# Full-array products in attention, a seven-product down projection, and a split join in a two-layer mixer block

## What is computed

```
p = modulate(rms_norm(x)) @ w_in                 # split into branches A, B, C, D and gates
A: grouped attention, 8 query heads of 64 on 2 key/value heads, rotary positions
B: latent attention, 8 heads, keys and queries of 64 + 32 columns, values of 64
C: a recurrent scan (WKV), forward and backward, computed in chunks of 64 tokens
D: 8 heads of 64, neighbourhood attention with a bias among latents, plus the context
   scores = q @ k^T * scale;  p = softmax(scores);  o = p @ v          # in A, B and D
x = x + gate1 * (sum_i sigmoid(g_i) * (o_i @ w_branch_i)) @ w_out
x = x + gate2 * (relu(modulate(rms_norm(x)) @ w_mlp1) ** 2) @ w_mlp2
```

## Time and profile before

| | us |
|---|---|
| median of 3 runs | 2406.4 (2401.82 to 2408.03) |
| profiled execution | 2408.26 |
| its span, first to last instruction | 2406.5 |
| TensorE busy | 2362.7 |
| VectorE busy | 1075.4 |
| ScalarE busy | 602.9 |
| GpSimd busy | 348.2 |

### The profile page before, as it was taken

The page is one execution under the profiler, slowest core; times in us unless marked ns, Lnnn a source line. Parts: engine busy times, 40 slices in busy tenths (PEclk is TensorE's granted clock), DMA queues, the critical chain, the costliest instruction groups (busy, mean ns, idle before and its releaser), DMA issues.

```text
span 2406.5 us, 48804 instructions
## 1 busy us (share of the span) xinstructions
PE 2362.7 (98%) x21774; PEld 1617.1 (67%) x21774; DVE 1075.4 (45%) x1988; ACT 602.9 (25%) x1248; POOL 348.2 (14%) x249
## 2 busy tenths in 40 slices
PE   8999999999999999999999999999999999999998
PEld 5554564455556554458888887566577767788887
DVE  3452334243555542137876875431546566421101
ACT  3353323132232321011000002441333334211100
POOL 0000000000101100026666671010000011000000
PEclk9999999999999999999999999999999999999999
DMA  8101111213231113232224565112121212245443
GB/s 307 53 18 70 45 61 44 96 63 110 95 107 39 45 46 115 78 123 97 88 88 149 189 243 194 53 71 89 53 89 64 64 61 66 81 149 175 155 152 105
DMA packets 64543, 239.99 MB, mean 100 GB/s; under 512 B 7024, under 2 KB 8064, under 8 KB 63440
## 3 DMA queue, kind: packets, MB, share of 16 engines
q1 hardware_dynamic: 61824, 220.23, 26.6%
q0 software_dynamic: 2512, 16.66, 1.9%
HBM read 235.81 MB, written 1.05 MB: 98 GB/s over the span
## 4 chain that ended last, share of the span: by engine, by line
PE 89%; DVE 5%; DMA 2%; issue 1%; ACT 1%; SPq 0%; DVEq 0%; ACTq 0%
PE psum L430 87%; PE psum L769 2%; DMA normed<-panels 1%; DVE normed L2348 1%; DVE normed L2345 1%; DMA arena<-panels 1%; DVE arena L2329 0%; SPq L2712 0%; ACT arena L811 0%; DVE arena L1492 0%; ACT normed L719 0%; ACT arena L821 0%; DVE arena L1509 0%; DVE arena L1507 0%; DVE arena L1235 0%
## 5 line engine op out<-in xcount | busy, mean ns | idle before, releaser
L430 PE MATMUL psum<-normed,panel_ring 128*128 128x256 f32 (+1 forms) x2880 | 973.5, 484 | 3.0 <-DVE arena L1235 1.1
L430 PEld LDWEIGHTS psum<-normed,panel_ring 128*128 128x128 f32 x2880 | 530.2, 190 | 318.9 <-issue 265.8
L430 PE MATMUL psum<-arena 64*64 64x64 f32 (+6 forms) x14040 | 608.2, 251 | 20.1 <-issue 9.0
L430 PEld LDWEIGHTS psum<-arena 64*64 64x64 f32 (+3 forms) x14040 | 431.6, 139 | 251.6 <-issue 180.9
L430 PE MATMUL psum<-arena,panel_ring 128*128 128x256 f32 (+1 forms) x2048 | 550.4, 422 | 0.0
L430 PEld LDWEIGHTS psum<-arena,panel_ring 128*128 128x128 f32 x2048 | 384.3, 190 | 125.2 <-issue 81.4
L786 DVE TENSOR_REDUCE softmax_stats<-psum 128x1 f32<-128x512 f32 (+1 forms) x144 | 83.7, 599 | 171.6 <-PE psum L430 170.3
L811 ACT ACTIVATE arena<-psum,softmax_stats 128x512 f32<-128x512 f32 (+1 forms) x144 | 87.6, 612 | 211.8 <-PE psum L769 102.5
L1235 DVE SCALAR_TENSOR_TENSOR arena<-arena,psum 128x512 f32<-128x512 f32 (+1 forms) x64 | 35.3, 553 | 152.8 <-PE psum L430 145.3
L1220 ACT ACTIVATE arena<-psum 128x512 f32<-128x512 f32 (+1 forms) x64 | 31.4, 490 | 216.1 <-PE psum L430 216.0
L1728 POOL COPY arena<-arena 128x512 f32<-128x512 f32 x16 | 21.3, 1356 | 440.8 <-PE psum L430 431.1
(11 more groups left out here) (215 smaller groups left out, 1872.5 us busy)
## 6 DMA issues: line engine op xcount, KB each, us to landing
panel_ring<-panels SPq DMA_DIRECT2D x350, 512.0 KB, 3.5
normed<-panels SPq DMA_DIRECT2D x40, 512.0 KB, 3.7
arena<-panels SPq DMA_DIRECT2D x24, 512.0 KB, 12.0
arena<-small_b POOLq DMA_DIRECT2D x2, 2176.0 KB, 8.9
arena<-bias_d POOLq DMA_DIRECT2D x2, 2048.0 KB, 8.9
arena<-x_t SPq DMA_DIRECT2D x2, 1024.0 KB, 7.1
arena<-x_t POOLq DMA_DIRECT2D x1, 2048.0 KB, 10.6
arena<-const_r POOLq DMA_DIRECT2D x2, 800.0 KB, 6.3
```

What stands on the lines that cost most here:

```text
L430: return nc.tensor.matmul(out, lhsT, rhs, start=start, stop=stop, skip_group_check=check)
```

## The change

1. Attention. The keys of A and the queries of D exist twice, once with zeros in the rows of head 1 and once with zeros in those of head 0 (`a_k1`, `d_q1`), and a score product runs over all 128 rows. VectorE makes A's second key in the normalisation stage; ScalarE makes D's two query tiles with a per-partition scale (`head_scale`) that is zero in one half. The two value products of a key tile become one, with both heads' value columns as stationary side and both heads' probabilities as 512 moving columns; of its result each head's own quarter is copied out, by two VectorE copies. B's scores stay as they are.
2. Down projection of layer 1 (`stage_mlp_down7` for `stage_mlp`). The up projection stays. The hidden tiles are laid out as 16 groups of seven parts; 16 units of two panels each have 7 x 4 products of 128 columns. GpSimd makes three weight sums of a unit, VectorE two; a join of four output quarters follows every fourth unit.
3. Branch C. The join has one step more: state products of one kind, a yield, state products of the other kind, `h_full`, and then the products for the outputs. In the plan half of a step's fillers are placed before the neighbouring pair's `close` and `prep` instructions.

```diff
-                        for i in range(2):
-                            p = mm(psum[heads[i], 4 + g % 2, :CTX], v_of(t, i, kt), probT[:, g % 2, i, kt, :], kt == 0, kt == nk // P - 1)
+                        p = mm(psum[:, 4 + g % 2, :], v_of(t, kt), probT[:, g % 2, :, kt, :], kt == 0, kt == nk // P - 1)
...
-                    nc.vector.tensor_copy(out[:, t, half * CTX - col0:(half + 1) * CTX - col0], psum[:, 4 + g % 2, :CTX]).then_inc(out_free.h, 1)
+                    for i in range(2):
+                        p = nc.vector.tensor_copy(out[heads[i], t, half * CTX - col0:(half + 1) * CTX - col0],
+                                                  psum[heads[i], 4 + g % 2, i * CTX:(i + 1) * CTX])
+                    p.then_inc(out_free.h, 1)
...
+                if s == 0:
+                    nc.vector.memset(other[:64, :], 0.0)
...
+                    if j == 1:
+                        nc.vector.tensor_copy(other[64:, :CTX], k[64:, :CTX])
+                        nc.vector.tensor_tensor(t[:64], t[:64], turned[:64], ALU.add)
+                        link(e, nc.vector.tensor_tensor(other[64:, CTX:], t[64:], turned[64:], ALU.add))
+                        nc.vector.memset(k[64:, :], 0.0).then_inc(rotated.h, 1)
...
-                    nc.scalar.activation(q[:, j, :], ps[:, :nq], ACT.Copy, scale=HD ** -0.5).then_inc(b.free.h, 1)
+                    if j == 0:
+                        e.wait_ge(rotated[0].h, rotated[0].at(rotated[1]))
+                        e.wait_ge(up_done[0].h, up_done[0].at(up_done[1]))
+                    nc.scalar.activation(q[:, j, :], ps[:, :nq], ACT.Identity, scale=head_scale[0])
+                    nc.scalar.activation(at["d_q1"][:, j, :], ps[:, :nq], ACT.Identity, scale=head_scale[1]).then_inc(b.free.h, 1)
...
-            e.wait_ge(gq_ready.h, gq_ready.at(1))
-            for c in y_chunks:
-                for d, hd in units:
-                    t = tside(d, hd)
-                    mm(yb[d][half[hd], token(c)], pu[t, d, c, 1, :], m4[t, d, c, :], False, False, check=True)
             for n, (src, right) in enumerate(((kt, vt), (bt, pu[:, :, :, 1, :]))):
+                if n == 0:
+                    e.wait_ge(gq_ready.h, gq_ready.at(1))
...
-            p.then_inc(h_full.h, 1)
-            yield
+                if n == 1:
+                    p.then_inc(h_full.h, 1)
+                    for c in y_chunks:
+                        for d, hd in units:
+                            t = tside(d, hd)
+                            mm(yb[d][half[hd], token(c)], pu[t, d, c, 1, :], m4[t, d, c, :], False, False, check=True)
+                yield
...
+                between = n // 2 if (p and tick < CLOSE) or (p < PAIRS - 1 and tick > RAW + LEVEL_STEPS) else 0
+                fill(others, between)
...
-                fill(others, n)
+                fill(others, n - between)
```

The core of the new down projection, TensorE's part of a unit and the sums that it waits for:

```diff
+                e.wait_ge(weights.h, weights.at(3 * u + 1))
+                product(u, bank(v, 0)[:, 1, :], x2, 0, opens(u))
+                e.wait_ge(shared.h, shared.at(2 * u + 1))
+                product(u, bank(v, 1)[:, 0, :], x5, 3, opens(u))
+                p = product(u, bank(v, 0)[:, 0, :], w1[:, 0:4, :], 1, False, begins=True)
...
+                e.wait_ge(shared.h, shared.at(2 * u + 2))
+                product(u, bank(v, 2)[:, 0, :], w1[:, 4:8, :], 6, opens(u))
+                e.wait_ge(weights.h, weights.at(3 * u + 3))
+                p = product(u, bank(v, 1)[:, 1, :], w2[:, 4:8, :], 2, False, begins=True)
...
+                p = product(u, bank(v, 2)[:, 1, :], w2[:, 0:4, :], 5, False)
...
+                product(u, m1_bank(v), x1, 4, opens(u)).then_inc(m1_done.h, 1)
...
+            if u >= 2:
+                e.wait_ge(m1_done.h, m1_done.at(u - 1))
...
+                nc.gpsimd.tensor_tensor(wx[:, u % 2, 1], w2[:, 0:4, :], w2[:, 4:8, :], ALU.add).then_inc(weights.h, 1)
+                nc.gpsimd.tensor_tensor(w2[:, 0:4, :], w2[:, 0:4, :], w1[:, 0:4, :], ALU.subtract).then_inc(weights.h, 1)
+                nc.gpsimd.tensor_tensor(wx[:, u % 2, 0], w1[:, 0:4, :], w2[:, 4:8, :], ALU.add).then_inc(weights.h, 1)
...
+                nc.vector.tensor_tensor(wx[:, u % 2, 2], w1[:, 0:4, :], w1[:, 4:8, :], ALU.add).then_inc(shared.h, 1)
+                e.wait_ge(shared.h, shared.at(2 * u + 1))
+                nc.vector.tensor_tensor(w1[:, 4:8, :], w1[:, 4:8, :], w2[:, 4:8, :], ALU.subtract).then_inc(shared.h, 1)
```

More of the change, by code:

```diff
@@ L371, in build @@
     eps, gn_eps = gc[:, G_EPS:G_EPS + 1], gc[:, G_EPS + 1:G_EPS + 2]
+    head_scale = [gc[:, G_EPS + 2 + i:G_EPS + 3 + i] for i in range(2)]
     def carve(at, *shape):
@@ L1980, in pe, with product @@
-            sum_up(e)
+            def product(u, out, lhs, part, opening, begins=False):
+                for k in range(4):
+                    p = mm(out, lhs[:, k, :], hid[:, 4 * (u % 4) + k, part, :], opening and k == 0, closes(u) and k == 3, check=True)
+                    if begins and k == 0:
+                        p.then_inc(panels_begun.h, 1)
+                return p
+            for u in range(NU):
+                at_first = P_DOWN + 8 * (u // 4) + u % 4
+                loaded[u] = stream.take(l, at_first), stream.take(l, at_first + 4)
@@ new lines, in pe, with arrived @@
+            e.wait_ge(added.h, added.at(KT - 3))
+            token_sums(6, h[:, 0, tok], n, True)
+            e.wait_ge(squared.h, squared.at(KT - 1))
+            token_sums(6, h[:, KT - 2, tok], n, False)
+            e.wait_ge(squared.h, squared.at(KT))
+            token_sums(6, h[:, KT - 1, tok], n, False).then_inc(sums_full.h, 1)
+            yield
+        def arrived(e, u):
+            for _, slot_in, n_in in loaded[u]:
+                e.wait_ge(slot_in.h, n_in)
+            if u >= 2:
+                e.wait_ge(m1_done.h, m1_done.at(u - 1))
@@ new lines, in pool @@
+        def pool(e):
+            yield from idle(8 * N_UP)
+            for u in range(NU):
+                (w1, _, _), (w2, _, _) = loaded[u]
+                arrived(e, u)
+                nc.gpsimd.tensor_tensor(wx[:, u % 2, 1], w2[:, 0:4, :], w2[:, 4:8, :], ALU.add).then_inc(weights.h, 1)
+                nc.gpsimd.tensor_tensor(w2[:, 0:4, :], w2[:, 0:4, :], w1[:, 0:4, :], ALU.subtract).then_inc(weights.h, 1)
+                nc.gpsimd.tensor_tensor(wx[:, u % 2, 0], w1[:, 0:4, :], w2[:, 4:8, :], ALU.add).then_inc(weights.h, 1)
+                yield
@@ L2003, in dve, with residual_of @@
+                if j in (29, 31):
+                    weight_sums((j - 29) // 2)
                 yield
             e.wait_ge(mod_ready[l].h, mod_ready[l].at(4))
-            for m in range(KT):
-                if m >= 2:
-                    add(e, m - 1)
-                residual(e, outs, m, l, lambda m, s: mod[:, l, 40 + m, s:s + 1], tok, None)
+            def residual_of(m, s, c):
+                return nc.vector.scalar_tensor_tensor(x[:, m, (left, right)[s]], c, mod[:, l, 40 + m, 1:2], x[:, m, (left, right)[s]],
+                                                      ALU.mult, ALU.add)
@@ L2009, in dve @@
+            for u in range(NU):
+                if closes(u) and u == NU - 1:
+                    join(u // 4)
+                if u + 2 < NU:
+                    weight_sums(u + 2)
+                if closes(u) and u < NU - 1:
+                    join(u // 4)
                 yield
             yield
-        return Stage(f"mlp{l}", 8 * N_UP + KT + 1, pe=pe, act=act, dve=dve), sums_full, (outs.full, KT)
+        return Stage(f"mlp{l}", 8 * N_UP + NU + 1, pe=pe, act=act, dve=dve, pool=pool), sums_full, (emptied, ND)
@@ L2021, in stage_mlp7 @@
         inputs, weights, m1_done, hid_ready = (sem("mlp_" + a, t) for a, t in (
[L2022 removed]
+            ("vector_sums", 5), ("weights", 10 * NU), ("m1_done", 2 * NU), ("hidden", NU)))
         m3_full, m4_full, m67_full, m3_copied, m67_copied, emptied = (sem("mlp7_" + a, NU + ND) for a in (
@@ L2640, in layer @@
         else:
-            stage, sums, loadable = stage_mlp(l, tok, at["hid"], at["relu"], ready, at["rstd"])
+            stage, sums, loadable = stage_mlp_down7(l, tok, at, ready)
             place(stage, 12)
```

146 lines of the change are left out of this document (112 added, 34 removed).

## The result

The changed kernel takes 2465.7 us (median of 4 runs, 2461.66 to 2470.15) against 2407.2 for the kernel before (4 runs): +58.5 us, ratio 1.0248, 95% interval 1.0225 to 1.0272. The forecast was 2457 us in a range of 2446 to 2468. The time lies in the range. It is 8.7 us above the forecast, and +58.5 us over the kernel before where the forecast's sum gave +48.8.

A forecast was written before the change was run, and what follows sets the result against it. TensorE's instruction stream was taken as the bound, busy 2362.7 of 2406.5 us. Terms 61.5 + 1 - 3 - 9.95 + 0.7 - 1.5 = +48.8 us on the profiled 2408.3 gave 2457 us, range 2446 to 2468.

The forecast's parts named there:

- attention, from whole cycles: Attention of both layers: full products instead of packed pairs lengthen the cycles of A, B and D, +61.5 us in sum.
- normalisation stage's extra instructions: Normalisation before attention, both layers: work queued behind A's second-key memsets delays TensorE, +1 us (0 to 4).
- waits that the longer stream fills: Attention, above all A: the longer TensorE stream fills idle gaps, 1.7 us in each layer, -3 us (0 to -6).
- down projection with its tail: Layer 1: 896 narrower records instead of 110.55 us give -9.95 us, the longer tail +0.7 us.
- split join, fillers in between: Branch C: both edits remove waits of TensorE at the scan and in the merges, -1.5 us (-5 to +3).
- the tail: After layer 1's down projection: the last join's added additions and residuals delay the last square, +0.7 us (0 to +1.5).
- The rival of binding weight sums: Down projection of layer 1: GpSimd's sums at 2.25 us each set the pace, +10.5 us, 2468 us; chance 0.12.
- nearly as now: Branch C: TensorE's waits at the scan's state update, 3.2 us before, were to stay about the same.
- the likeliest case alone: Whole kernel: the forecast with its own terms' bounds and no rival, 2450 to 2464 us; chance 0.74.

The follow-up runs named there:

- e8: The changed kernel without the split join and without the fillers in between: 2463.9 us, ratio 1.0249 to the kernel before.
- e10: The changed kernel with its split join but with the fillers placed as before: 2457.5 us, ratio 1.0223 to the kernel before.
- e4: The kernel before with the split join and the fillers in between, together and alone: 2409.9 us, ratio 1.0023.
- e2: The kernel before with the zero-padded scores of A and D alone, values still packed pairs: 2424.5 us, ratio 1.0086.
- e5: The kernel before with only the two loops around the packed value products swapped, all of head 0 first: 2424.6 us, ratio 1.0085.
- e1: The kernel before with the value products alone as full products, scores still packed pairs: 2458.3 us, ratio 1.0220.
- e3: The kernel before with the seven-product down projection of layer 1 alone: 2398.1 us, ratio 0.9969.
- e11: The kernel before with the seven-product down projection, all five weight sums of a unit on GpSimd: 2390.4 us in one run.
- e6: The kernel before with the split join and its added step alone, fillers placed as before: 2404.6 us, ratio 1.0001.
- e7: The kernel before with half of a step's fillers placed before the neighbour pair's instructions, join as before: 2414.7 us, ratio 1.0038.

## Why the prediction was right, and where it was off

| step | predicted us | measured us |
|---|---|---|
| attention, from whole cycles | +61.5 | +61.8 (e8, stages +36.0 and +25.8), all three rows together; +60.9 in e10 |
| normalisation stage's extra instructions | +1 | not seen: 52.0 us from the first norm of layer 1 to the first row maximum, before 52.1 |
| waits that the longer stream fills | -3 | -0.3 (waits for the exponentials, 1.2 before, 0.9 after) |
| down projection with its tail | -9.25 | -9.2 (the whole last stage) |
| split join, fillers in between | -1.5 | +3 to +8 (e4) |
| sum | +48.8 | +57.1 (spans), +58.5 (medians) |

**Attention.** The mechanism is shown, not only argued. A pair of products in different halves of the array overlaps in time, and a full product does not make up for it: the cycles of D and B came out at 30.10 and 30.13 us in layer 0, 17.21 and 12.95 in layer 1, against the forecast 30.11, 30.11, 17.21 and 12.93; e2 shows that zeros save nothing, e5 that the gain lies in the order of the stream. Pricing whole cycles instead of single stretches was what made it exact, since the entries and exits of the packed stretches were thus in the sum: ten fillers take 4.39 us before a packed score (e1, 416.37 to 420.76) and 4.29 before a full one (e1, 259.40 to 263.69), and four transposes 0.49 behind a packed stretch and 0.44 behind a full one. The change saved these, and they are small beside what it lost. The Trainium skill's page TensorEngine Tiling (Array Packing), Key Properties, says that a change of tiling mode drains the engine, without a figure. The 0.1 us agree with it in kind; that they are this drain no run here shows.

**The waits that would be filled** were filled by 0.3 us instead of 3, a miss of 2.7 us. One wait of 0.32 us in A of layer 1 is gone (1535.42 before). The cycle of A in layer 0, where TensorE waits for ScalarE's exponentials, still has its two, 0.57 and 0.29 us before, 0.61 and 0.30 after; the first of them before, then both after:

```profile
123.70 3.01 PE L430 MATMUL psum<-arena 64*128 64x512 f32 x20 [0.57 <-ACT arena L811]
```

```profile
125.84 5.42 PE L433 MATMUL psum<-arena 128*128 128x512 f32 x12 [0.61 <-ACT arena L816]
...
147.85 5.42 PE L433 MATMUL psum<-arena 128*128 128x512 f32 x12 [0.30 <-ACT arena L816]
```

The cycle went from 18.37 to 22.01 us, +3.64, even more than the 3.44 of D. A score product waits until the exponentials of the item before it are done. From the start of that item's scores to the end of the first wait it was 4.01 us before (119.69 to 123.70) and 4.23 after (121.61 to 125.84): the chain grew by 0.22 us, and the scores at its head by 0.23 (0.63 to 0.86). A longer product fills a wait only if it does not lie on the chain that is waited for, and here it did. Nor were all of the 1.7 us of gaps that the term was taken from such waits: 0.57 and 0.29 are, another 0.55 in the same 60 us waits for L1050, a square in branch B.

**The down projection** was right in sum: the body gave 0.5 us more than forecast (100.6 forecast, 100.05 measured), and the tail took a little more (+0.7 forecast, +0.9 to the last square, +1.1 to the square root of the final norm). The row of another stage with the same shape, 0.1123 us a record, carried over to 0.6% (0.1117). The rival of binding weight sums fell, in e3 and, in its hard form, in e11.

**The split join and the fillers** is the step that failed in sign: "I take -1.5 us", measured +3 to +8 (e4). The prediction looked at the waits which the edits might remove, and not at the stage whose instructions they move: with the fillers split, half of the cover that stood behind the next pair's preparation went in front of it. e6 has the join at -2 to +2 us, e7 the fillers at +6 to +12, and in e10, which undoes them in the changed kernel, the stretch with attention of layer 1 is 2.9 us shorter. The waits at the scan's state update, forecast "nearly as now", went from 3.2 to 6.1 us in the changed kernel. The prediction's upper bound for this term was +3. That the total still fell into the range owes something to the range's width, 2446 to 2468, which had been opened upwards for the weight sums, a rival that did not come; the likeliest case alone ended at 2464, under the measured 2465.7.

**What stays open:** how much of the fillers' cost is waits at the tanh (3.4 us in e7's span) and how much spells of lower clock in the first pair; what the join itself costs within 2 us; and why e8, without the join, is 6 us slower by the medians than e10 with it, where e6 finds no effect of the join. The intervals of e8 and e10 overlap, and of the 5.4 us between their profiled spans 3.9 lie ahead of the second norm of layer 0, 1.1 in the MLP of layer 0 and 0.5 in layer 1; the first of these stretches varies as much without an edit.

## What to carry to other kernels

Where TensorE is the bound, two products of half the rows or half the columns in different halves of the array are worth keeping: here a full product with zeros, or with a half that is thrown away, cost 1.4 to 1.8 times a packed pair (0.86 us against 0.63 for scores at 256 keys, 3.44 against 1.88 for values at 512). Price such a change on whole cycles of the steady state, with unchanged work inside, and transfer a record's pace only between equal shapes. Fillers have a side: moving them before an instruction takes them from behind it. Here that brought back waits of 1.1 us at a time and cost 6 to 12 us in all, not all of which was traced.

## What the runs showed of the hardware

- Packed products need not alternate one by one. Two 256-column products of one half (four records), then two of the other, cost 3.74 us a stretch against 3.69 in strict alternation; four and four cost 4.60, serial would be 5.16.
- Products of 96 and of 128 rows pace at 0.43 us a record of 512 columns alike, and so does the padded score, of whose 128 rows 64 are zeros.
- A GpSimd sum of 128x512 starts every 1.23 us in an undisturbed unit of e11. With VectorE's weight sums beside them (e3) the three take 1.64, 1.63 and 1.33 us in the mean, single ones up to 1.8 (2.25 in layer 0), and VectorE's second sum 1.64. Moving two of five sums to VectorE bought GpSimd only 1.5 us a unit (4.6 against 6.1).
